# Small first loads and a four-part output store in a two-network block on one core

## The chip, the cores and the metric

The kernel runs on one core of one Trainium2 chip. The metric is the time of one execution in microseconds (us) on the device; the time of a version is the median of its runs. Names of engines in the profile: PE is TensorE's matmuls, PEld its weight loads, DVE is VectorE, ACT is ScalarE, POOL is GpSimd, SP is SyncE, which here issues all DMAs.

## The reference

The input x is 256 tokens by 1024 features, in float32. It goes through ten residual sublayers of one network and eight of a second one. Only the first and the last step matter for this change:

```python
for layer in range(2):
    x = x + 0.5 * swiglu(rmsnorm(x, ffn1_norm[layer]), ffn1_w_in[layer], ffn1_w_out[layer])
    ...                      # mixer (attention with a linear recurrence, then a delta rule),
                             # cross attention to a memory of 256 tokens, second swiglu
x = rmsnorm(x, final_norm)
for i in range(4):           # second network: retention, conformer convolution, GLA, retention
    ...
    h = h + rmsnorm_2(sq_relu_mlp(u, mlp_w_up[i], mlp_w_down[i]), norm_gains[i, 3])
```

swiglu is `(silu(gate) * up) @ w_out` with `gate, up = split(h @ w_in)`; rmsnorm divides by the root of the mean square over the features and multiplies by a gain. The first weight that is read is therefore `ffn1_w_in[0]`, the first gains are `ffn1_norm[0]`, and the last thing computed is x plus a normed MLP output.

## The kernel before, in words

**Layout.** Activations stand transposed: features on the 128 partitions, 8 chunks of 256 tokens side by side, so that x is one tile `X` of 128x2048 (chunk c is columns 256c to 256c+255). All weights are one list of 836 tiles of 128x1024, each made of four blocks of 128x256 in the order in which TensorE wants them. Tile t is loaded by SP into `SL[t % 3]`.

**Split precision.** Each product is made of three float32r products. ScalarE copies a tile to its rounded high part `WH[t % 4]` (`hi(t)`, L1981 to L1986), VectorE subtracts that from the original and gets the low part `WL[t % 4]` (`lo(t)`, L946 to L950). Activations are split likewise: `high` on ScalarE (L2053) and `low` on VectorE (L1012). TensorE takes block by block: high x high, high x low, low x high, each for two halves of 128 columns, six matmuls a block and 24 a tile (`multiply`, L293).

**Waits.** `tile` (L287) lets TensorE wait for `s_lo`, once every four blocks. `hi(t)` waits for the tile's DMA and, from the fifth tile on, for TensorE to be through with tile t-4. SP may load tile t when `lo(t-3)` is done. So the first three tiles have free buffers, and tile 3 is issued after `lo(0)`.

**Order of the start.** The first stage, `f1.0.in`, has 22 output groups of 8 blocks. Its first three groups are interleaved: for each chunk k of the input, blocks of groups 0, 1 and 2 (24 blocks, six tiles); from group 3 on the groups follow one another. ScalarE and VectorE run `walk_new` with n = 0 (L1999, L963): for each chunk c the split of the input chunk, and ahead of each even c one weight tile (tiles 0 to 3). Then the squares of the input for the norm (`square`, `add_squares`), and then `walk`, which handles tile b/4+3 at every fourth block b, so tile 4 comes right after the squares. Ahead of block (3, 0) TensorE sums the squares over the partitions (`total`), then ScalarE takes the root as exp(-0.5 ln) (`root`, L2041), for which `logs()` (L2021) loads an activation table. From there VectorE and ScalarE evaluate the swiglu groups as they are finished. Ahead of block (6, 0) TensorE transposes the memory (`mem_transposes`, L395) into three small banks in four lots; ScalarE empties these in `mem_copies` (L2157) when its own list has come there.

**Queues.** There is no planner: every engine has a list written out by hand. SP issues, in this order, the table of gains, biases and constants `PK` (128x1189, 594.5 KB), columns 0 to 1023 of x, weight tile 0, columns 1024 to 2047 of x, tiles 1 and 2, the memory (1 MB), then tiles 3 and 4, the positions, the constants `CP`, and the rest of the tiles (L2764 to L2783). TensorE, VectorE and ScalarE each wait for all of `PK` ahead of their first work (L914, L1962, L2718). At the end VectorE adds the last normed output to x chunk by chunk (`post_norm`, L1053), and SP waits for chunk 7, stores all of `X` with one DMA of 1 MB and waits for it (L2784 to L2786).

Of the kernel before, what the change touches and what calls it, by code (L numbers as in the profile page):

```python
# [109 lines left out]
def build_program(nc, w, pk, cp, xT_in, mem_in, pos_in, out):  # L110
    F32 = mybir.dt.float32
    I32 = mybir.dt.int32
    F32R = mybir.dt.float32r
    ALU = mybir.AluOpType
# [9 lines left out]
    with ctx:  # L124
# [47 lines left out]

        s_w = [sem(f"s_w{i}") for i in range(NRAW)]
        s_pk, s_mem, s_pos, s_cp, s_o = (sem(n) for n in ("s_pk", "s_mem", "s_pos", "s_cp", "s_o"))
        s_x = [sem(f"s_x{i}") for i in range(2)]
        s_hi, s_lo = sem("s_hi"), sem("s_lo")
        s_block, s_small = sem("s_block"), sem("s_small")
        s_bank = [sem(f"s_bank{i}") for i in range(8)]
# [81 lines left out]
        def tensor_program(p):  # L260
# [25 lines left out]

            def tile(st, j, k):  # L287
                b = st.at(j, k)
                if b % 4 == 0:
                    p.wait_ge(s_lo, b // 4 + 1)  # L290
                return WH[b // 4 % 4], WL[b // 4 % 4], b % 4 * 256

# [100 lines left out]
                to_x(f + ".out", 8 if n == 7 else None, RB, R03, hid_lo, f)  # L393

            def mem_transposes():  # L395
                p.wait_ge(s_mem, 16)
                for tb in range(2):
                    for q in range(2):
                        bk = small(("mem", tb, q))
                        for c in range(4):  # L400
                            at = tb * 1024 + (4 * q + c) * 128
                            t = p.transpose(bk[:, c * 128:(c + 1) * 128], PG[4][:, at:at + 128], IDN)
                        t.then_inc(s_small, 1)
# [507 lines left out]
                to_x("g.o", 18, R45, R45, o_lo, "g", 0, 2048)  # L911
                total(18)

            p.wait_ge(s_pk, 16)  # L914
            p.wait_ge(ones.sem, ones["ones"])
            for layer in range(2):
                n = 4 * layer
# [27 lines left out]
        def vector_program(v):  # L945
            def lo(t):  # L946
                if t < NTILES:
                    v.wait_ge(s_hi, t + 1)
                    v.tensor_tensor(WL[t % NSPL][:, :], SL[t % NRAW][:, :], WH[t % NSPL][:, :].bitcast(F32),  # L949
                                    ALU.subtract).then_inc(s_lo, 1)  # L950

            def walk(name, n=None, skip=0):

                st = ST[name]
                for x, (j, k) in enumerate(st.order):
                    b = st.block + x * st.width
                    if b and b % 4 == 0 and x >= skip:
                        lo(b // 4 + 3)
                    yield j, k
                    if n is not None and not st.outer and (j, k) == (0, 3):  # L960
                        add_squares(n, 3)

            def walk_new(name, n, chunk):  # L963

                t = ST[name].block // 4 + 3
                if n == 0:
                    for c in range(8):
                        if c % 2 == 0:
                            lo(c // 2)
                        chunk(c)  # L970
                else:
                    for c in range(8):
                        chunk(c, t + c // 2 - 2 if c in (4, 6) else None)
                    lo(t + 2)
                add_squares(n, 1)
                add_squares(n, 2)
                if n:
                    lo(t + 3)
                add_squares(n, 3)
                for j, k in walk(name, None, 16 if n else 0):  # L980
                    yield j, k
# [105 lines left out]
            def swiglu(f, n, gain, chunk=None):  # L1087
                name = f + ".in"
                for j, k in (walk(name, n) if n else walk_new(name, n, chunk)):
                    if n == 0 and (j, k) == (9, 3):  # L1090
                        mem_scaled()
                    for x in due(name, j, k, n > 0):
                        if x == 0:
                            v.wait_ge(s_rst, n + 1)
                        u = x // 2
                        s = Y8[:, u % 2 * 512:u % 2 * 512 + 512]
                        d = PG[10][:, u % 4 * 512:u % 4 * 512 + 512]
                        bk, free = done(name, x)
                        if x % 2 == 0:
                            v.tensor_tensor(r3(s), r3(bk[:, :]), RB2, ALU.mult).then_inc(free, 1)  # L1100
                            if u:
                                hid_low(f, u - 1)
                            continue
                        v.tensor_tensor(r3(d), r3(bk[:, :]), RB2, ALU.mult).then_inc(free, 1)
                        evacuated(name, x)
                        v.wait_ge(silu.sem, silu[f, u])
                        v.tensor_tensor(d, d, s, ALU.mult).then_inc(hid.sem, hid.give((f, u)))  # L1107
                hid_low(f, 10)
                if n == 7:
                    for j, k in walk(f + ".out"):  # L1110
                        rotary(0, j, k)
                        out_group(f + ".out", j, k, 8, 0.5, None)
                    return
                add_to_x(f + ".out", n + 1, 0.5, gain)
# [844 lines left out]
                return post_norm(18, 2, 1, gain)  # L1959

            v.memset(ONES[:, :], 1.0).then_inc(ones.sem, ones.give("ones"))
            v.wait_ge(s_pk, 16)  # L1962
            for layer in range(2):
                n = 4 * layer
                swiglu(f"f1.{layer}", n, gains("mix", 8 * layer), lambda c: low(0, c, gains("ffn1")))
# [14 lines left out]
        def scalar_program(a):  # L1980
            def hi(t):  # L1981
                if t < NTILES:
# [2 lines left out]
                        a.wait_ge(s_block, 4 * (t - NSPL + 1))  # L1985
                    a.activation(WH[t % NSPL][:, :], SL[t % NRAW][:, :], ACT.Copy).then_inc(s_hi, 1)  # L1986

            def walk(name, n=None, skip=0):

                st = ST[name]  # L1990
                for x, (j, k) in enumerate(st.order):
                    b = st.block + x * st.width
                    if b and b % 4 == 0 and x >= skip:
                        hi(b // 4 + 3)
                    yield j, k
                    if n is not None and (j, k) == ((3, 0) if st.outer else (0, 7)):
                        root(n)

            def walk_new(name, n, chunk):  # L1999

                t = ST[name].block // 4 + 3
                for c in range(8):
                    if n == 0 and c % 2 == 0:
                        hi(c // 2)
                    if n and c in (4, 6):
                        hi(t + c // 2 - 2)
                    chunk(c)
                square(n, 0, X[:, hc(0)])
                square(n, 1, X[:, hc(1)])
                if n:  # L2010
                    hi(t + 2)
                square(n, 2, X[:, hc(2)])
                square(n, 3, X[:, hc(3)])
                if n:
                    hi(t + 3)
                for x, (j, k) in enumerate(walk(name, n, 16 if n else 0)):
                    if n == 17 and x in (16, 20):
                        whole(n, range(x - 16, x - 12), gains("ng", 64))
                    yield j, k
# [20 lines left out]

            def root(n):  # L2041
                to = 258 if n in TOK else 256
                if n < 8:
                    logs()
                a.wait_ge(s_sums, n + 1)
                a.activation(RST[:, 0:to], BK[7][:, 0:to], ACT.Ln, bias=pc("eps"), scale=1.0 / 1024).then_inc(s_bank[7], 1)  # L2046
                a.wait_ge(s_bank[7], n + 1)
                a.activation(RST[:, 0:to], RST[:, 0:to], ACT.Exp, scale=-0.5).then_inc(s_rst, 1)
# [80 lines left out]

            def first_norm():  # L2130
                def chunk(c):
                    if c in (0, 4):
                        a.wait_ge(s_x[c // 4], 16)
                    high(0, c, gains("ffn1"))
                return chunk

# [578 lines left out]
                    pass  # L2715
                return post_norm(18, gain)

            a.wait_ge(s_pk, 16)  # L2718
            chunk = first_norm()
            for layer in range(2):  # L2720
                n = 4 * layer
# [5 lines left out]
            for i in range(4):  # L2727
                gain = gains("ng", (4 * i + 2) * 8)
                if i % 3 == 0:
                    chunk = retention(i, gain, chunk)  # L2730
                else:
                    chunk = (conformer, gla)[i - 1](gain, chunk)
                chunk = mlp(i, gains("ng", (4 * i + 4) * 8) if i < 3 else None, chunk)

        def sync_program(s):
            T0 = ST["dn.k"].block // 4
# [24 lines left out]
                    for b in range(8):  # L2761
                        s.dma_start(diagonal((PG[5], PG[4])[x], b), apart(DY, b, 256 * x)).then_inc(s_dn_y[x], 16)

            s.dma_start(PK[:, :], pk).then_inc(s_pk, 16)  # L2764
            s.dma_start(X[:, 0:1024], xT_in[:, 0:1024]).then_inc(s_x[0], 16)
            again = {ST["f2.0.in"].block // 4 + 8: (1, "xo0"), ST["f2.1.in"].block // 4 + 8: (2, "xo1"),
                     ST["m1.up"].block // 4 + 8: (3, "r0.o"), ST["m2.up"].block // 4 + 8: (2, "g.o")}
            for t in range(NTILES):
# [4 lines left out]
                blocks_of_16(t)  # L2773
                if t >= NRAW:
                    s.wait_ge(s_lo, t - NRAW + 1)
                s.dma_start(SL[t % NRAW][:, :], w[t]).then_inc(s_w[t % NRAW], 16)
                if t == 0:
                    s.dma_start(X[:, 1024:2048], xT_in[:, 1024:2048]).then_inc(s_x[1], 16)
                if t == 2:
                    s.dma_start(PG[4][:, :], mem_in[0]).then_inc(s_mem, 16)  # L2780
                if t == 4:
                    s.dma_start(POS[:, :], pos_in).then_inc(s_pos, 16)
                    s.dma_start(CP[:, :], cp[0]).then_inc(s_cp, 16)  # L2783
            s.wait_ge(xn.sem, xn[NN - 1, 7])  # L2784
            s.dma_start(out, X[:, :]).then_inc(s_o, 16)
            s.wait_ge(s_o, 16)  # L2786

        block_ = ctx.enter_context(nc.Block())

# [169 lines left out]
```

## Time and profile before

| | us |
|---|---|
| median of three runs | 2836.77 |
| the three runs | 2827.97, 2836.77, 2836.91 |
| span of the profiled execution, first to last instruction | 2834.6 |
| PE busy / DVE busy / ACT busy in that span | 2717.1 / 1812.7 / 1411.2 |

The profiled execution's own time is known only as its span; the median of the runs lies 2.2 us above it. TensorE is busy in 96% of the span, so time is made or lost in the few places where it stands idle, and at both ends. "Busy" of PE does not say at which clock it runs; the granted clock, 1.00 for full, is a separate column. In the profile a row's "idle before" names how long the engine stood idle and whose work ended that.

### The profile page before, as it was taken

How to read it: one execution, taken by the hardware profiler on the slowest of the kernel's cores; microseconds unless marked ns; L12 is line 12 of the kernel's file. 1: busy time of each engine (PE TensorE's matmuls, PEld its weight loads, DVE VectorE, ACT ScalarE, POOL GpSimd, SP SyncE). 2: the span in 40 equal slices, each digit the busy share in tenths (PEclk: the TensorE clock that was granted, in tenths of full speed). 3: DMA queues.
4: the chain of work that ended last, by engine and by line, in shares of the span. 5: the costliest groups of instructions: out<-in, count | busy, mean ns of one | idle time of the engine just before them, and what ended most of it. 6: DMA issues, size and time to landing. Idle time of an engine off the chain costs nothing. (4 is left out here: it accounts for less than half of the span.)

```text
span 2834.6 us, 49287 instructions
## 1 busy us (share of the span) xinstructions
PE 2717.1 (96%) x21142; PEld 2620.1 (92%) x21142; DVE 1812.7 (64%) x2351; ACT 1411.2 (50%) x1928; POOL 0.2 (0%) x4
## 2 busy tenths in 40 slices
PE   7999999999998899999999999989999999999998
PEld 7999899999987889999999999979988899989998
DVE  5658656656657746666746855967554685755764
ACT  5445545454456354545446565354454544446443
POOL 0000000000000000000000000000000000000000
PEclk9999999999999999999999999999999999999999
DMA  6554535555543133555544454135542455444463
GB/s 215 178 186 142 176 123 190 191 182 188 182 147 120 68 121 135 180 189 169 179 149 149 166 193 170 68 96 184 193 149 97 149 197 188 155 163 148 151 200 127
DMA packets 129002, 450.13 MB, mean 159 GB/s; under 512 B 20112, under 2 KB 20368, under 8 KB 128528
## 3 DMA queue, kind: packets, MB, share of 16 engines
q1 hardware_dynamic: 128784, 446.96, 47.0%
q8 instruction: 168, 2.75, 0.4%
q14 instruction: 50, 0.41, 0.0%
HBM read 445.47 MB, written 1.44 MB: 158 GB/s over the span
## 5 line engine op out<-in xcount | busy, mean ns | idle before, releaser
L262 PE MATMUL B<-R,WH 128*128 128x256 f32 x10432 | 2089.1, 283 | 45.5 <-DVE WL L949 28.4
L262 PEld LDWEIGHTS B<-R,WH 128*128 128x128 f32 x10432 | 1674.9, 189 | 63.6 <-issue 25.4
L949 DVE TENSOR_TENSOR WL<-SL,WH 128x1024 fp32r<-128x1024 f32 x836 | 1011.0, 1223 | 769.3 <-ACT WH L1986 768.1
L262 PE MATMUL B<-R,WL 128*128 128x256 f32 x4480 | 1255.1, 280 | 0.0
L1986 ACT ACTIVATE WH<-SL 128x1024 fp32r<-128x1024 f32 x836 | 865.9, 1052 | 567.5 <-PE B L262 442.5
L262 PEld LDWEIGHTS B<-R,WL 128*128 128x128 f32 x4480 | 845.7, 189 | 0.0
L262 PE MATMUL B<-RB,WH 128*128 128x256 f32 x1984 | 555.0, 280 | 0.0
L262 PE MATMUL B<-RB,WL 128*128 128x256 f32 x1728 | 482.7, 279 | 0.0
L262 PEld LDWEIGHTS B<-RB,WH 128*128 128x128 f32 x1984 | 372.2, 188 | 0.4
L262 PEld LDWEIGHTS B<-RB,WL 128*128 128x128 f32 x1728 | 323.8, 187 | 0.0
L262 PE MATMUL B<-WH,R 128*128 128x512 f32 x480 | 160.3, 403 | 1.3 <-DVE WL L949 1.3
L262 PE MATMUL B<-PG 128*128 128x256 f32 (+6 forms) x672 | 129.6, 337 | 8.8 <-DVE PG L1437 3.8
L262 PEld LDWEIGHTS B<-PG 128*128 128x128 f32 (+2 forms) x672 | 105.9, 187 | 22.8 <-issue 4.8
L2495 ACT ACTIVATE RB<-PG 128x512 fp32r<-128x512 f32 x64 | 40.5, 633 | 159.7 <-DVE PG L1583 159.7
L2054 ACT ACTIVATE R<-X,PK 128x256 fp32r<-128x256 f32 x128 | 61.4, 505 | 116.0 <-DVE X L1023 63.4
L262 PEld LDWEIGHTS B<-WH,R 128*128 128x128 f32 x480 | 90.7, 189 | 27.4 <-issue 3.5
L262 PE MATMUL B<-PG,ONES 128*128 128x256 f32 (+1 forms) x242 | 72.5, 422 | 30.7 <-DVE PG L990 15.0
L262 PE MATMUL B<-WL,R 128*128 128x512 f32 x240 | 95.2, 397 | 0.0
L2150 ACT ACTIVATE RB<-PG 128x512 fp32r<-128x512 f32 x44 | 27.8, 632 | 129.2 <-DVE PG L1107 129.2
L262 PEld LDWEIGHTS B<-PG,ONES 128*128 128x128 f32 x242 | 42.6, 195 | 41.0 <-issue 24.3
L1015 DVE SCALAR_TENSOR_TENSOR R<-X,PK,R 128x256 fp32r<-128x256 f32 x128 | 59.0, 482 | 28.7 <-ACT R L2054 28.7
L1038 DVE TENSOR_TENSOR R<-PG,RB 128x512 fp32r<-128x512 f32 x108 | 73.9, 685 | 3.3 <-ACT RB L2150 2.8
(282 smaller groups left out, 1541.2 us busy)
## 6 DMA issues: line engine op xcount, KB each, us to landing
SL<-in_w SPq DMA_DIRECT2D x836, 512.0 KB, 3.5
CP<-in_cp SPq DMA_DIRECT2D x5, 768.0 KB, 5.7
X<-in_xT SPq DMA_DIRECT2D x2, 512.0 KB, 6.9
PG<-in_mem SPq DMA_DIRECT2D x1, 1024.0 KB, 11.2
out<-X SPq DMA_DIRECT2D x1, 1024.0 KB, 3.9
PK<-in_pk SPq DMA_DIRECT2D x1, 594.5 KB, 3.8
dn_y<-PG SPq DMA_DIRECT2D x1, 256.0 KB, 2.3
PG<-dn_y SPq DMA_DIRECT2D x16, 16.0 KB, 2.2
```

The source lines that it names most:

```text
L262: return p.matmul(o, left, right, start=first, stop=final, skip_group_check=True)
L949: v.tensor_tensor(WL[t % NSPL][:, :], SL[t % NRAW][:, :], WH[t % NSPL][:, :].bitcast(F32), ALU.subtract).then_inc(s_lo, 1)
L1015: v.scalar_tensor_tensor(R67[:, 2048 + c * 256:2304 + c * 256], X[:, cc(c)], gain(c), R67[:, cc(c)].bitcast(F32), ALU.mult, ALU.subtract). ...
L1038: v.tensor_tensor(R03[:, hc(u)], d, RB[:, hc(u)].bitcast(F32), ALU.subtract).then_inc(hid_lo.sem, hid_lo.give((f, u)))
L1986: a.activation(WH[t % NSPL][:, :], SL[t % NRAW][:, :], ACT.Copy).then_inc(s_hi, 1)
L2054: a.activation(R67[:, cc(c)], X[:, cc(c)], ACT.Copy, scale=gain(c)).then_inc(h_hi.sem, h_hi.give((n, c)))
L2150: a.activation(RB[:, hc(u)], PG[10][:, u % 4 * 512:u % 4 * 512 + 512], ACT.Copy).then_inc(hid_hi.sem, hid_hi.give((f, u)))
L2495: a.activation(RB[:, hc(x)], PG[10][:, x % 4 * 512:x % 4 * 512 + 512], ACT.Copy).then_inc(hid_hi.sem, hid_hi.give((f, x)))
```

## The change

The first loads are cut up and put in another order, the waits for them with them, and the output is stored in four parts.

- SP first loads block 0 of tile 0 (128x256, 128 KB), then the 16 columns of `PK` that hold the first norm's gains (8 KB), then the other three blocks of tile 0 (384 KB), tile 1, the second half of x, tile 2, the rest of `PK`, the memory.
- ScalarE issues three DMAs itself, for chunk 0, chunk 1 and chunks 2 and 3 of x, then loads the logarithm's activation table (`logs()`), then waits for the gains. `root(0)` no longer loads that table.
- Tile 0 is split in two parts, block 0 and blocks 1 to 3, each with its own high and low instruction; TensorE waits for `s_lo_first` ahead of block 0, and for `s_lo` ahead of block 1.
- The waits for all of `PK` move to where its other columns are read: `mem_transposes`, `root(0)`, and VectorE's first `swiglu` group.
- The output goes in four DMAs, chunks 0 to 3, 4 and 5, 6, and 7, each when its last chunk is added.

```diff
@@ tensor_program @@
-                if b % 4 == 0:
+                if b == 0:
+                    p.wait_ge(s_lo_first, 1)
+                elif b == 1 or b % 4 == 0:
                     p.wait_ge(s_lo, b // 4 + 1)
...
             def mem_transposes():
+                p.wait_ge(s_pk, 16)
                 p.wait_ge(s_mem, 16)
...
-            p.wait_ge(s_pk, 16)
             p.wait_ge(ones.sem, ones["ones"])
@@ vector_program @@
+            def lo_part(part, needs, gives):
+                v.wait_ge(needs, 1)
+                v.tensor_tensor(WL[0][:, part], SL[0][:, part], WH[0][:, part].bitcast(F32), ALU.subtract).then_inc(gives, 1)
...
                 if n == 0:
-                    for c in range(8):
+                    lo_part(slice(0, 256), s_hi_first, s_lo_first)
+                    chunk(0)
+                    lo_part(slice(256, 1024), s_hi, s_lo)
+                    chunk(1)
+                    for c in range(2, 8):
                         if c % 2 == 0:
                             lo(c // 2)
                         chunk(c)
...
                             v.wait_ge(s_rst, n + 1)
+                            if n == 0:
+                                v.wait_ge(s_pk, 16)
...
-            v.wait_ge(s_pk, 16)
+            v.wait_ge(s_gain, 16)
@@ scalar_program @@
+            def hi_part(part, needs, gives):
+                a.wait_ge(needs, 16)
+                a.activation(WH[0][:, part], SL[0][:, part], ACT.Copy).then_inc(gives, 1)
...
+                if n == 0:
+                    hi_part(slice(0, 256), s_w_first, s_hi_first)
                 for c in range(8):
-                    if n == 0 and c % 2 == 0:
+                    if n == 0 and c == 1:
+                        hi_part(slice(256, 1024), s_w[0], s_hi)
+                    if n == 0 and c and c % 2 == 0:
                         hi(c // 2)
...
-                if n < 8:
+                if 0 < n < 8:
                     logs()
+                if n == 0:
+                    a.wait_ge(s_pk, 16)
...
-                    if c in (0, 4):
-                        a.wait_ge(s_x[c // 4], 16)
+                    if c in (0, 1, 2, 4):
+                        a.wait_ge(s_x[(0, 1, 2, 4).index(c)], 16)
...
-            a.wait_ge(s_pk, 16)
+            for x in range(3):
+                at = slice(XCUT[x], XCUT[x + 1])          # XCUT = (0, 256, 512, 1024, 2048)
+                a.dma_start(X[:, at], xT_in[:, at]).then_inc(s_x[x], 16)
+            logs()
+            a.wait_ge(s_gain, 16)
@@ sync_program @@
-            s.dma_start(PK[:, :], pk).then_inc(s_pk, 16)
-            s.dma_start(X[:, 0:1024], xT_in[:, 0:1024]).then_inc(s_x[0], 16)
+            s.dma_start(SL[0][:, 0:256], w[0][:, 0:256]).then_inc(s_w_first, 16)
+            s.dma_start(PK[:, 0:16], pk[:, 0:16]).then_inc(s_gain, 16)
+            s.dma_start(SL[0][:, 256:1024], w[0][:, 256:1024]).then_inc(s_w[0], 16)
...
-                s.dma_start(SL[t % NRAW][:, :], w[t]).then_inc(s_w[t % NRAW], 16)
-                if t == 0:
-                    s.dma_start(X[:, 1024:2048], xT_in[:, 1024:2048]).then_inc(s_x[1], 16)
+                if t:
+                    s.dma_start(SL[t % NRAW][:, :], w[t]).then_inc(s_w[t % NRAW], 16)
+                if t == 1:
+                    s.dma_start(X[:, 1024:2048], xT_in[:, 1024:2048]).then_inc(s_x[3], 16)
                 if t == 2:
+                    s.dma_start(PK[:, 16:NPK], pk[:, 16:NPK]).then_inc(s_pk, 16)
                     s.dma_start(PG[4][:, :], mem_in[0]).then_inc(s_mem, 16)
...
-            s.wait_ge(xn.sem, xn[NN - 1, 7])
-            s.dma_start(out, X[:, :]).then_inc(s_o, 16)
-            s.wait_ge(s_o, 16)
+            for c0, c1 in OUT:                            # OUT = ((0, 4), (4, 6), (6, 7), (7, 8))
+                s.wait_ge(xn.sem, xn[NN - 1, c1 - 1])
+                s.dma_start(out[:, c0 * 256:c1 * 256], X[:, c0 * 256:c1 * 256]).then_inc(s_o, 16)
+            s.wait_ge(s_o, 16 * len(OUT))
```

## Rows read from the trace of the kernel before

**Rows 1.** The page, part 1: busy us, share of the span, instructions.

```profile
PE 2717.1 (96%) x21142; PEld 2620.1 (92%) x21142; DVE 1812.7 (64%) x2351; ACT 1411.2 (50%) x1928; POOL 0.2 (0%) x4
```

**Rows 2.** Waits, whole span: waiter, releaser, us in total, times, longest.

```profile
PE B L262 <- DVE WL L949: 29.6, 27, 12.7
...
PE B L402 <- ACT PG L2161: 4.3, 1, 4.3
```

**Rows 3.** Timeline of SP's start: start us, us, what, [idle before <-releaser].

```profile
0.73 0.38 SPq L2764 DMA_DIRECT2D PK<-in_pk  x1
...
3.93 0.50 SPq L2780 DMA_DIRECT2D PG<-in_mem  x1
12.56 2.26 SPq L2776 DMA_DIRECT2D SL<-in_w  x2
```

**Rows 4.** Timeline of ACT, 0 to 54 us.

```profile
8.85 1.28 ACT L1986 ACT_TABLE_LOAD   x1 [8.85 <-DMA SL<-in_w]
...
17.05 1.06 ACT L1986 ACTIVATE WH<-SL 128x1024 fp32r<-128x1024 f32 x1 [1.56 <-DMA SL<-in_w]
...
20.90 1.05 ACT L1986 ACTIVATE WH<-SL 128x1024 fp32r<-128x1024 f32 x1
...
32.75 1.28 ACT L2022 ACT_TABLE_LOAD   x1
34.05 0.47 ACT L2046 ACTIVATE RST<-B,PK 128x256 f32<-128x256 f32 x1
...
53.97 1.55 ACT L2161 ACTIVATE PG<-B 128x512 f32<-128x512 f32 x3
```

**Rows 5.** Timeline of DVE, 22 to 52 us.

```profile
22.73 1.22 DVE L949 TENSOR_TENSOR WL<-SL,WH 128x1024 fp32r<-128x1024 f32 x1
...
51.05 0.68 DVE L1104 TENSOR_TENSOR PG<-B,RST 128x512 f32<-128x512 f32 x1
```

**Rows 6.** Timeline of PE, 22 to 55 us.

```profile
22.94 0.40 PE L262 MATMUL B<-R,WH 128*128 128x256 f32 x2
...
31.42 0.59 PE L262 MATMUL B<-PG,ONES 128*128 128x256 f32 x2
...
54.60 1.12 PE L402 MATMUL B<-PK,PG 128*128 128x128 f32 x4 [4.32 <-ACT PG L2161]
```

**Rows 7.** Stretches: length, busy (instructions) by engine, granted PE clock, DMA share, GB/s.

```profile
12.00:16.45 4.45, 3.77 (x18) 3.80 (x19) 4.45 (x8) 3.49 (x7) 0.00 (x0) 1.00 0.89 338
22.00:50.00 28.00, 28.00 (x239) 27.95 (x238) 18.62 (x22) 16.75 (x19) 0.00 (x0) 1.00 0.56 186
...
1043.00:1047.00 4.00, 4.00 (x24) 4.00 (x23) 1.97 (x5) 1.93 (x3) 0.00 (x0) 0.61 0.37 131
```

**Rows 8.** Stretches of one us, same columns.

```profile
13.00:14.00 1.00, 1.00 (x6) 1.00 (x6) 1.00 (x2) 1.00 (x3) 0.00 (x0) 1.00 0.70 279
```

**Rows 9.** The page, part 6: KB of one DMA, median us from issue to landing.

```profile
PG<-in_mem SPq DMA_DIRECT2D x1, 1024.0 KB, 11.2
out<-X SPq DMA_DIRECT2D x1, 1024.0 KB, 3.9
...
dn_y<-PG SPq DMA_DIRECT2D x1, 256.0 KB, 2.3
PG<-dn_y SPq DMA_DIRECT2D x16, 16.0 KB, 2.2
```

**Rows 10.** Weight tiles' DMAs in the first 40 us.

```profile
DMA to landing us min/median/max: 3.4/4.3/9.3
```

**Rows 11.** Timeline of DVE and SP at the end.

```profile
2829.89 0.42 DVE L1063 TENSOR_TENSOR X<-X,PG 128x256 f32<-128x256 f32 x1
2830.35 0.34 SPq L2785 DMA_DIRECT2D out<-X  x1
```

**Rows 12.** Timeline of PE, two later idle times.

```profile
1042.75 0.50 PE L262 MATMUL B<-R,WH 128*128 128x256 f32 x2 [2.18 <-DVE WL L949]
...
2222.99 0.46 PE L262 MATMUL B<-PG,ONES 128*128 128x256 f32 x1 [3.00 <-DVE PG L990]
```

More of the change, by code:

```diff
@@ L174, in build_program @@
         s_pk, s_mem, s_pos, s_cp, s_o = (sem(n) for n in ("s_pk", "s_mem", "s_pos", "s_cp", "s_o"))
-        s_x = [sem(f"s_x{i}") for i in range(2)]
+        s_x = [sem(f"s_x{i}") for i in range(4)]
+        XCUT = (0, 256, 512, 1024, 2048)
+        s_gain, s_w_first, s_hi_first, s_lo_first = (sem(n) for n in ("s_gain", "s_w_first", "s_hi_first", "s_lo_first"))
         s_hi, s_lo = sem("s_hi"), sem("s_lo")
@@ L2733, in scalar_program @@
                 chunk = mlp(i, gains("ng", (4 * i + 4) * 8) if i < 3 else None, chunk)
+        OUT = ((0, 4), (4, 6), (6, 7), (7, 8))
         def sync_program(s):
```

## The prediction

> **What bounds the kernel now.** I read the busy shares first [rows 1]: TensorE is busy for 2717.1 of 2834.6 us, so at most 117 us are to be had from its idle time, and both ends of the kernel are part of that. The waits come next [rows 2]: 29.6 us are spent waiting for VectorE's low parts of weights, and the longest of those waits, 12.7 us, is the start; the other 26 share 17 us and the change does not touch them. The one wait for ScalarE's copies of the transposed memory (L402) costs 4.3 us and matters below. Then the timelines of each engine at both ends.
>
> At the start the reader should see two things. TensorE begins at 12.7, because ScalarE waits until 8.85 for tile 0, behind the 594.5 KB of PK and half of x, and then loads a table for 1.28 us that nobody needs to wait for [rows 3, 4]. And once it has begun, it is never short of weights until 50 us (28.00 us busy in 28.00) [rows 7]. So the question is how soon TensorE would run short if it began sooner.
>
> **The start: how much of the earlier begin is kept.** When does it begin? The smallest loads of the trace land 2.2 to 2.3 us after issue [rows 9]. SP's first issue stands at 0.73 [rows 3]; block 0, the gains and chunk 0 should be there near 3.5. ScalarE's three issues (0.4 us each, as SP's) and the table load end near 3.3, so the load is hidden. High part, low part and the input's split of 128x256 are about 0.5 us each: first matmul near 5, one block, then a pause for blocks 1 to 3. These wait for 384 KB behind the small pieces, near 6.5, and for about 0.8 us of high and 0.9 us of low part (three quarters of 1.06 and 1.22): near 8.5. So TensorE begins 4 us earlier for good, by its own inputs.
>
> When does it run short? Weight tile 3 can't come much sooner. It stands behind the same 4.3 MB as before (PK, x, tiles 0 to 2, memory): the memory landed at 3.93 + 11.2 = 15.1 [rows 3, 9], and tile 3, issued at 12.56 after lo(0), was taken up by ScalarE at 17.05, on arrival [rows 3, 4]. What changes is that lo(0) is done about 4 us earlier, so tile 3 is queued right behind the memory; in the microsecond after 13 the DMAs showed a dip to 0.70 of their share [rows 8], which that closes. I take 0.5 us for it; the bounds are -1 (small rows and a second queue cost more than the dip) and +1.1 (12.56 + 3.4 = 15.96, the fastest landing of a tile in this stretch [rows 10]).
>
> Behind tile 3 there is a fixed list. ScalarE does hi(3), two input chunks, four squares, hi(4); VectorE does lo(3), two chunks, the sums of squares, lo(4), which ends at 22.73 + 1.22 = 23.95, that is 6.9 us after hi(3) started [rows 4, 5]. VectorE was without a pause in it. So lo(4) ends at 23.95 - 0.5 = 23.45 in the new kernel whatever TensorE does. TensorE began tile 3 at 22.94 and the sums at 31.42, three tiles later [rows 6]: 2.83 us each, and tile 4 at 25.77. In the new kernel, from block 1 at 8.5: about 3.8 us at half rate, as now (18 matmuls in 3.77 us, against 239 in 28.00 [rows 7]; the granted clock reads 1.00 in that first stretch, but 0.21 us a matmul against 0.117 is the engine's lower level, 1.2 of 2.4 GHz), then full rate, tile 3 would be wanted at 18.2; lo(3), 2.3 us behind its hi, is there near 18.9. Tile 4 would be wanted at 21.7 and is there at 23.45. From there tiles 5 and up were ready 2.7 us and more ahead of their use, so TensorE isn't held again. Gain at the start: 25.77 - 23.45 = **2.3 us**, not the 4 to 8 of the earlier begin. It doesn't depend on the exact begin: blocks 1 to 3 could start at 10 and tile 4 would still be waited for. Bounds 0.8 and 2.9 from those of tile 3. Cutting tile 0's high and low parts in two adds a fixed cost of some 0.3 us to each engine before 9, hidden in the wait for tile 3.
>
> **The table load.** root(0) loses the load at 32.75: the logarithm ran at 34.05 [rows 4], so it can start 1.30 us sooner, measured from TensorE's sums. From there ScalarE and VectorE work one behind the other and behind TensorE until 54 us: group 5 is scaled by VectorE at 51.05 [rows 5], while TensorE had finished it (it is the last before the transposes) near 49. The copies start at 53.97 [rows 4] and free the bank that TensorE has waited for for 4.32 us [rows 6]. No step of that chain waits for TensorE or a load by less than 1.3 us, as far as I follow it, so the whole **1.3 us** comes off this wait. Bounds 0 (one such wait found) and 1.3. After 54.6 everything follows TensorE again. No new load replaces it, since copies and squares need none of their own: at the end squares and the logarithm run with one table.
>
> On its price the Trainium skill differs (ScalarE: Activation LUTs, "What ACT_TABLE_LOAD costs"): it gives 1.28 us for the load and 1.38 for a drain, 2.66 in all. The trace shows the load and no drain: 32.75 to 34.05. By the page the term would be 2.7, by the trace 1.3.
>
> **Waits for PK** move behind 586 KB loaded before the memory, thus there before 15; their users come at 32 (root), 33 (first group) and 49. Cost nothing; if PK came after the memory instead, still nothing. Behind the moved wait on ScalarE stand root and all copies of weights, so only a landing past 32 would cost.
>
> **The end.** VectorE adds chunk 7 at 2829.89; the store is issued at 2830.35 and lands 3.9 us later [rows 9, 11], near the end of the span. Each chunk takes VectorE 0.86 us, so parts 1 to 3 are issued 3.4, 1.7 and 0.86 us before the last; an issue costs 0.34, so SP is free for each. The last part is 128 KB. 256 KB landed in 2.3 us, 16 KB in 2.2 [rows 9]: I take 2.3, so **1.6 us** less. Bounds: 0.5 (3.4, the fastest half megabyte [rows 10]) and 1.7.
>
> Of that the Trainium skill says (DMA: Bandwidth & Descriptors, "Anatomy of one DMA"), for another issuing path, that a DMA takes 2.0 us plus its bytes at 436 GB/s: 4.4 us for 1 MB, 2.3 for 128 KB, which would be a term of 2.1; the trace's 3.9 is below that. Its advice to batch DMAs speaks against small pieces; this is weighed in the bound of -1 above.
>
> **Sum.** 2.3 + 1.3 + 1.6 = 5.2 us: span 2834.6 - 5.2 = 2829.4, and with the 2.2 us between span and median 2836.77 - 5.2 = **2831.6**. About 0.3%, 8.5 us, is what a measurement of this kernel can tell from no change: its own three runs spread over 8.9 us. So the forecast is a gain inside that bound.
>
> **Rivals.**
> (a) Supply sooner: the DMAs moved 279 GB/s in the dip and 338 around it [rows 7, 8], and could run faster in the new order, so that tile 3 lands before 15 and TensorE sets its own pace: tile 4 at 21.7, start gain 4.1, in all 7.0: 2829.8. Against: the same bytes stand ahead. Chance 0.12.
> (b) The clock falls in the new pauses. TensorE now pauses near 18.5 and, for 1.7 us, before 23.45. After an idle time of 2.18 us at 1042.75 the granted clock read 0.61 in the next 4 us, with 24 matmuls where 34 fit [rows 7, 12]: 1.2 us lost there, 1.6 with its edges. This would leave 0.7 of the start's 2.3: 2833.2. For: the pauses are of that length; against: 3.00 us of idle at 2222.99 were followed by full pace (matmuls 0.117 apart), so idle time alone doesn't decide. Chance 0.2. The Trainium skill (TensorE: Matmul & The Clock Gate, Part 1) has the same two levels and says that the point at which the clock changes varies from run to run, which no single trace can show.
> (c) The pieces land no sooner than before, or the load stays: only the end's 1.6 and part of the rest, 2834. Chance 0.1.
> (d) Slower: the same gate further on. Everything after 55 us comes 3.6 us earlier, and in this execution about six idle times of 1.8 us or more went without a fall (2222.99 is one) while six others brought one. Each that changes sides costs 1.6, as above, to 2.8, the longest of the trace. From four more on (6.4 to 11) the gain is used up: 2838 to 2843. It must be a majority in one direction, and just as likely the other way. Chance 0.08.
> The forecast itself keeps 0.5.
>
> **Numbers.** One run of three lay 8.9 us below the others, which (d)'s mechanism would explain (five falls fewer), and it may strike the new kernel too. A median of three lands in the low state with 3 x (1/3)^2 x (2/3) + (1/3)^3 = 0.26, giving 2823. So faster by over 0.3%: 0.25 (this, and a little of (a)); slower by over 0.3%: 0.04 from (d); within: 0.71. Range 2822 to 2838: the low state below, (c) and the light end of (d) above; the forecast's own range, from the bounds of the three terms (1.3 to 5.9), is 2830.9 to 2835.5.
>
> **What would show it.** First matmul near 5, dense from 8 to 9. ScalarE takes tile 3 at 16 to 17, waiting for its DMA. A TensorE wait of 1 to 2 us for lo(4) near 22 to 23.5, none before the transposes. The logarithm right behind hi(9), and the wait at L402 down from 4.3 to 3.0. Last store landing 2.2 to 2.4 after issue. Wrong if tile 4 isn't waited for (then (a)), if matmuls near 20 to 28 stand 0.21 apart (b), or if L402's wait stays at 4.3.

## The result and the profile after

Over 20 runs of each, the changed kernel took 2832.53 us in the median (2816.96 to 2839.08) and the kernel before 2838.94 (2827.97 to 2848.4). The ratio is 0.9977, with a 95% interval of 0.9966 to 0.9988: 6.5 us less, between 3.4 and 9.7. The forecast was 5.2 us less. Both the sign and the size came out, but one of the three terms, the start, did not, as this section and the experiments show.

The timeline of ScalarE in the changed kernel's first 55 us (start, duration, engine, line, operation, idle time before it and what ended that) shows the start:

```profile
2.12 1.28 ACT L2044 ACT_TABLE_LOAD   x1 [2.12 <-issue]
...
8.65 0.84 ACT L2004 ACTIVATE WH<-SL 128x768 fp32r<-128x768 f32 x1 [3.60 <-DMA SL<-in_w]
...
17.74 1.06 ACT L2000 ACTIVATE WH<-SL 128x1024 fp32r<-128x1024 f32 x1 [3.42 <-DMA SL<-in_w]
...
31.32 1.06 ACT L2000 ACTIVATE WH<-SL 128x1024 fp32r<-128x1024 f32 x1 [0.32 <-DMA SL<-in_w]
32.29 0.45 ACT L2070 ACTIVATE RST<-B,PK 128x256 f32<-128x256 f32 x1
```

The table load is out of the way at 3.4 and no second one precedes the logarithm, which starts right behind the high part of tile 9: both as forecast. But the rest of tile 0 was taken up at 8.65 (forecast 6.5), and tile 3 at 17.74, later than the 17.05 of before [rows 4] and not sooner. The last tile ahead of the root, tile 9, was waited for as well, at 31.32. Tile 3 was late, and the first loads had run slower than in the kernel before. The first seven microseconds, before and then changed (length, busy time and instructions of PE, PEld, DVE, ACT and POOL, granted clock, DMA share, GB/s):

```profile
0.00:7.00 7.00, 0.00 (x0) 0.00 (x0) 0.17 (x1) 0.00 (x0) 0.20 (x4) 1.00 0.67 208
```

```profile
0.00:7.00 7.00, 1.62 (x6) 1.36 (x6) 0.98 (x3) 2.10 (x3) 0.20 (x4) 1.00 0.54 155
```

53 GB/s less over 7 us are 0.37 MB; at the 407 to 413 GB/s that the DMAs moved between 13 and 19 us these cost 0.9 us. Tile 3 was late by 0.7 us, which is of that size. TensorE's timeline has the same points from its side:

```profile
5.34 0.55 PE L264 MATMUL B<-R,WH 128*128 128x256 f32 x1 [5.34 <-DVE WL L958]
10.54 0.79 PE L264 MATMUL B<-R,WH 128*128 128x256 f32 x2 [3.58 <-DVE WL L958]
...
24.69 0.50 PE L264 MATMUL B<-R,WH 128*128 128x256 f32 x2 [1.20 <-DVE WL L953]
52.83 1.12 PE L407 MATMUL B<-PK,PG 128*128 128x128 f32 x4 [3.52 <-ACT PG L2185]
```

It starts at 5.3 instead of 12.7, works densely from 10.5, pauses for tile 4 until 24.69 (forecast 23.45; it began that tile at 25.77 before), and goes on after the transposes at 52.83, against 54.60 [rows 6]: 1.8 us sooner, where 3.6 were forecast.

Why tile 9 was late although TensorE came sooner, SP's list shows. SP may load tile 9 when `lo(6)` is done, and `lo(6)` follows hi(6), for which TensorE need only be through with tile 2. So in this stretch the issue doesn't wait for TensorE. Its issue in the kernel before, and in the changed one:

```profile
27.18 0.33 SPq L2776 DMA_DIRECT2D SL<-in_w  x1
```

```profile
26.93 0.33 SPq L2808 DMA_DIRECT2D SL<-in_w  x1
```

It landed 4.3 us later before, at 31.5, just ahead of TensorE's release of hi(9) at 31.68, and 4.4 us later in the changed kernel, at 31.3. TensorE reached the sums 1.0 us sooner (30.45, against 31.42 [rows 6]), but tile 9 was issued only 0.25 us sooner.

At the end, VectorE's last sum, and what each size of store took to land (page, part 6, for that stretch):

```profile
2822.19 0.42 DVE L1075 TENSOR_TENSOR X<-X,PG 128x256 f32<-128x256 f32 x1
```

```profile
out<-X SPq DMA_DIRECT2D x1, 512.0 KB, 2.6
out<-X SPq DMA_DIRECT2D x1, 256.0 KB, 2.5
out<-X SPq DMA_DIRECT2D x2, 128.0 KB, 1.9
```

The span ends at 2824.9, 2.3 us after that sum; before it was 2834.6 - 2830.3 = 4.3 [rows 11]. So the store gave 2.0 (forecast 1.6): 128 KB land in 1.9 us, less than the 2.3 that I took from 256 KB.

1.8 and 2.0 make 3.8. The two profiled executions differ by 9.7. The other 5.9 lie between 54.6 and the last sum, where no instruction was changed. Most of it lies in places like this one, as stretches in the same columns, of the changed kernel and then of the kernel before:

```profile
1160.00:1280.00 120.00, 120.00 (x1062) 120.00 (x1061) 83.66 (x94) 58.33 (x67) 0.00 (x0) 1.00 0.60 197
```

```profile
1160.00:1280.00 120.00, 120.00 (x1021) 120.00 (x1021) 80.83 (x90) 55.74 (x66) 0.00 (x0) 1.00 0.55 182
```

TensorE is busy throughout in both, at a granted clock of 1.00, and yet does 4% more matmuls in one: 0.113 us apart instead of 0.1175. The changed kernel's profile holds 30 stretches of 10 us with 90 or 91 matmuls, the other none. That is chance or the change's doing; the experiments had to tell.

### The profile page after: what moved, and what is told of

It is laid out like the page before. It is cut to its first block and busy times, and to the rows that moved or that the text cites. A ratio compares the mean times of both kernels' runs of the same rounds, so it can differ in the third digit from the quotient of the medians.

```text
span 2824.9 us, 49296 instructions
## 1 busy us (share of the span) xinstructions
PE 2712.5 (96%) x21142; PEld 2614.1 (93%) x21142; DVE 1811.8 (64%) x2352; ACT 1409.3 (50%) x1928; POOL 0.2 (0%) x4
## 5 line engine op out<-in xcount | busy, mean ns | idle before, releaser
L264 PE MATMUL B<-PG,ONES 128*128 128x256 f32 (+1 forms) x242 | 73.4, 426 | 29.5 <-DVE PG L1002 13.7
L2174 ACT ACTIVATE RB<-PG 128x512 fp32r<-128x512 f32 x44 | 27.8, 632 | 128.8 <-DVE PG L1121 128.8
```

The costliest lines, as they stand in the source:

```text
L264: return p.matmul(o, left, right, start=first, stop=final, skip_group_check=True)
L2174: a.activation(RB[:, hc(u)], PG[10][:, u % 4 * 512:u % 4 * 512 + 512], ACT.Copy).then_inc(hid_hi.sem, hid_hi.give((f, u)))
```

## The experiments

Eleven experiments were run; three of them are repeats, two of the changed kernel and one of the cut loads alone. The first four shared one chip and one set of runs of the kernel before. The next four ran on another chip with a second set, and the last three on that chip with a third. Where two versions are compared by their mean times, the number after +- is one standard error.

**The four-part store alone**, on the kernel before:

```diff
-            s.wait_ge(xn.sem, xn[NN - 1, 7])
-            s.dma_start(out, X[:, :]).then_inc(s_o, 16)
+            for c0, c1 in OUT:
+                s.wait_ge(xn.sem, xn[NN - 1, c1 - 1])
+                s.dma_start(out[:, c0 * 256:c1 * 256], X[:, c0 * 256:c1 * 256]).then_inc(s_o, 16)
```

> The kernel before with only the four-part store. Theory (the three terms add up, each in its own place): from the end of VectorE's last sum to the end of the span 2.3 us instead of 4.3, so 2.0 less; nothing else moves: TensorE goes on after the transposes at 54.6, as before. Rival (small stores wait for one another, and the gain of the changed kernel's end came from elsewhere): 3 us or more from the last sum to the end. Whole kernel by the theory -2.0 us, far inside the spread of runs, which I expect to come from the middle of the kernel: two profiled executions differ there by up to 5 us in single stretches at full granted clock.

Measured: last sum ends at 2837.45, span 2839.8, so 2.35 us; restart after the transposes at 54.27. Ratio 0.9993 (0.9978 to 1.0008). The term is 2.0 us and stands by itself; the rival is out.

**The table load alone**, on the kernel before:

```diff
-                if n < 8:
+                if 0 < n < 8:
                     logs()
...
+            logs()
             a.wait_ge(s_pk, 16)
             chunk = first_norm()
```

> The kernel before, with the logarithm's table loaded at ScalarE's start and not again ahead of the first root. Theory A (the load's price is 1.3 us wherever no load of weights holds ScalarE there): TensorE's restart after the transposes at 54.60 - 1.3 = 53.3, its wait 3.0 instead of 4.3. In the changed kernel it was 0.7, because ScalarE waited 0.3 us for tile 9's DMA just ahead. And the table load at the start goes out of the way of tile 0's high part too: ScalarE's first high part at 8.9 instead of 10.15, TensorE's start 1.3 earlier at 11.4; by theory B (tile 4 is not waited for in the kernel before, 1.8 us of slack) that start is kept whole as well: restart at 52.0. If tile 3 and its list bind, restart stays near 52.0 to 53.3. Rival C (the load at the root was hidden): restart at 54.6 less only the start's shift. Whole kernel -1.3 to -2.6 us.

Measured: start at 11.03, and TensorE's restart in the row below at 52.59, between the 53.3 of theory A and the 52.0 of theory B, its wait 2.89; the logarithm at 32.06. Ratio 0.9987 (0.9976 to 0.9999).

```profile
52.59 0.66 PE L402 MATMUL B<-PK,PG 128*128 128x128 f32 x4 [2.89 <-ACT PG L2161]
```

One line moved gives 2.0 us at the restart. From the start of hi(9) to the logarithm it is 0.97 us (31.09 to 32.06) instead of 2.37 (31.68 to 34.05): 1.4 for the load. The other 0.6 is hi(9) itself, 31.09 instead of 31.68, released by TensorE in both. TensorE had begun 1.65 us sooner, but its matmuls stood 0.21 us apart until 17.1 instead of 16.45, so a part of that was lost. The 2.0 us are more than all that the changed kernel gained at the restart (1.8, and 1.1 to 1.4 in its two repeats): on top of the moved table load, the cut loads made the restart 0.2 to 1.0 us later, not sooner.

**The cut loads alone**: the changed kernel with the single store and with the load ahead of the first root.

```diff
-                if 0 < n < 8:
+                if n < 8:
                     logs()
...
-            for c0, c1 in OUT:
...
+            s.wait_ge(xn.sem, xn[NN - 1, 7])
+            s.dma_start(out, X[:, :]).then_inc(s_o, 16)
```

> The changed kernel with the single store of 1 MB and with the table loaded again ahead of the first root: the cut loads alone. Theory A (start's gain 1.1 us, set by tile 3's landing at 17.7 and the fixed list behind it): TensorE waits for tile 4 until 24.7; restart after the transposes at 54.60 - 1.1 = 53.5. Rival (the load at the root is hidden by the wait for tile 9, so it costs nothing): restart at 52.8, as in the changed kernel. End: 4.3 us from the last sum, as before. Whole kernel by A -1.1 us.

Measured: TensorE waits for tile 4 until 24.40, near A's 24.7, and the end takes 4.3 us as before. But the restart is at 54.48, neither 53.5 nor 52.8: the cut loads alone gain nothing there. ScalarE's timeline says why:

```profile
31.55 1.06 ACT L2000 ACTIVATE WH<-SL 128x1024 fp32r<-128x1024 f32 x1 [0.31 <-DMA SL<-in_w]
32.63 1.28 ACT L2044 ACT_TABLE_LOAD   x1
33.92 0.47 ACT L2070 ACTIVATE RST<-B,PK 128x256 f32<-128x256 f32 x1
```

The reader should see that the root stands behind tile 9's DMA, at the time at which it stood before behind TensorE (31.68). As long as tile 9 is issued at 27.1, an earlier TensorE gains nothing. The first timing gave 0.9985 (0.9970 to 1.0000); that is taken up below.

**Fewer bytes ahead of the tiles.** The changed kernel with the rest of PK after tile 4 and the memory after tile 6:

```diff
-                if t == 2:
+                if t == 4:
                     s.dma_start(PK[:, 16:NPK], pk[:, 16:NPK]).then_inc(s_pk, 16)
+                if t == 6:
                     s.dma_start(PG[4][:, :], mem_in[0]).then_inc(s_mem, 16)
-                if t == 4:
+                if t == 16:
                     s.dma_start(POS[:, :], pos_in).then_inc(s_pos, 16)
```

> The changed kernel with the rest of PK issued after tile 4, the memory after tile 6, and positions and CP after tile 16. Theory A (the bytes ahead of tile 3 set the start's gain): 1.6 MB less stand ahead of tile 3, some 4 us at 400 GB/s, so ScalarE takes it near 14, lo(4) ends near 21, TensorE isn't held at tile 4 and reaches it at its own pace, 16 blocks from 10.5 with 3.8 us at half rate: near 23.6; restart after the transposes near 51.5 to 52.0, 1 us sooner than the changed kernel's 52.83. Rival B (the list of ScalarE and VectorE binds, not the landing): lo(4) at 24.6 as now, restart at 52.8. Rival C (the later loads collide with tiles 5 to 9): waits of TensorE for low parts after tile 4, restart later than 52.8. Whole kernel by A -7.5 us against before.

Measured: tile 3 taken up at 13.84 without a wait, no pause at tile 4, restart at 51.55. Theory A for tile 3. But the logarithm only moved to 31.01, since the memory's 1 MB now lay ahead of tile 7:

```profile
27.55 1.06 ACT L2000 ACTIVATE WH<-SL 128x1024 fp32r<-128x1024 f32 x1 [4.04 <-DMA SL<-in_w]
```

Ratio 0.9969 (0.9957 to 0.9980). So the collision had moved, not gone, and the next kernel moved the memory past tile 9.

**The memory after tile 12**, positions and CP after tile 20 (the same edit with `t == 12` and `t == 20`):

> The changed kernel with the rest of PK issued after tile 4, the memory after tile 12, positions and CP after tile 20. Theory A (TensorE's restart after the transposes stands 20.55 us behind the first root's logarithm in every trace so far, and the logarithm stands right behind the high part of tile 9, which waits for that tile's DMA): without the memory's 1 MB among tiles 7 to 9, hi(9) is released by TensorE at about 27, the logarithm starts near 28, restart near 48.5 to 49.5, which is 3 to 4 us sooner than the changed kernel's 52.83; whole kernel 7 to 9 us below before. Rival B (the start's pace is TensorE's or VectorE's, not the loads'): restart at 51.5, as with the memory after tile 6. Rival C (the memory lands too late for the transposes): a TensorE wait ahead of the transposes.

Measured: in ScalarE's timeline, tile 9 now waits for TensorE, and the logarithm stands at 29.94:

```profile
28.98 1.06 ACT L2000 ACTIVATE WH<-SL 128x1024 fp32r<-128x1024 f32 x1 [1.40 <-PE B L264]
```

SP issues tile 9 3.9 us sooner than in the changed kernel, and it lands 4.7 us later, at 27.8, 1.2 us before TensorE is through:

```profile
23.07 0.33 SPq L2808 DMA_DIRECT2D SL<-in_w  x1
```

Restart at 50.48, 2.4 us sooner than in the changed kernel; I had said 3 to 4, since I had TensorE 2 us too early at that tile. Median 2830.87, ratio **0.9959** (0.9944 to 0.9974). By the means it is 12.4 us below before, +- 1.9. This is the lowest ratio of all, but its interval overlaps those of the memory after tile 6 and of both edits together. The edit moves three loads at once, the rest of PK, the memory, and the positions with CP; which of them counts was not separated.

**The gains as 128 columns** (512 bytes a partition instead of 64), profiled once:

```diff
-            s.dma_start(PK[:, 0:16], pk[:, 0:16]).then_inc(s_gain, 16)
+            s.dma_start(PK[:, 0:128], pk[:, 0:128]).then_inc(s_gain, 16)
```

> The changed kernel with the first gains loaded as 128 columns of PK (512 bytes a partition, 64 KB) instead of 16 (64 bytes, 8 KB). Theory A (the short rows hold up the queue: in the changed kernel the DMAs moved 93 and 162 GB/s between 3 and 5 us, against 337 and 225 before): the rest of tile 0 lands 1 us or more sooner than 8.65, first matmul near 4.5, dense from near 9.5. Rival B (another reason for the slow microseconds, the second queue or the first accesses): first high part near 4.3 to 5, dense from 10.2 to 10.5 as now. By both the restart stays near 52.8, as tile 9's DMA sets it.

Measured: the rest of tile 0 at 7.67 (8.65 in the changed kernel), dense work from 9.55, restart at 52.30. The DMAs moved 189 GB/s in the first 7 us instead of 155, and tile 3 was taken up at 16.61, so tile 4 began at 23.57 and the sums at 29.12, 2.3 us sooner than before: here the start's gain on TensorE is what was forecast. Yet hi(9) waited for tile 9's DMA until 30.75, only 0.9 us sooner than before, so that the restart had 0.9 us of these 2.3, and 1.4 from the table load. The stretches of the fifth microsecond, first of this kernel, then of the changed one:

```profile
4.00:5.00 1.00, 0.00 (x0) 0.00 (x0) 0.00 (x0) 0.52 (x2) 0.00 (x0) 1.00 0.92 310
```

```profile
4.00:5.00 1.00, 0.00 (x0) 0.00 (x0) 0.23 (x1) 0.76 (x2) 0.00 (x0) 1.00 0.53 162
```

That fits theory A, but the profiles with the narrow gains took up the rest of tile 0 anywhere from 8.13 to 8.65, and the combined kernel below, with the wide gains too, only at 8.46. One profile doesn't settle a difference of that size.

**The memory after tile 12 in the kernel before**, profiled once, with the whole PK and x as before:

> The kernel before with the memory issued after tile 12, positions and CP after tile 20. Theory A (in the kernel before hi(9) waits for TensorE, not for a load): restart after the transposes unchanged at 54.3 to 54.6, logarithm at 33.7 to 34.05. Rival B (fewer bytes help whatever the start): restart 2 to 4 us sooner.

Measured: restart 54.75, logarithm 34.20, tile 9 released by TensorE. Theory A: late memory is worth nothing without the early start. The early start (the cut loads) is worth nothing without the late memory. Together they brought the restart 2.4 us ahead of the changed kernel's and 2.1 ahead of that with the table load alone. The late memory with the old start and the moved table load was not run.

**The changed kernel again**, profiled once:

> The changed kernel once more, for the spread. Theory A (the middle's 5.9 us between the two profiled executions was chance: 30 stretches of 10 us with 90 or 91 matmuls where all other traces have 87 or 88): restart near 52.8, end 2.3 us behind the last sum, but a middle of 2780 to 2784 us with few such stretches, as in the four experiments so far. Rival B (the change itself makes them): again near 30 of them, starting after 1159 and 1928, and a middle near 2770.

Measured: restart 53.18, 2.3 us at the end, and between them 2778.8 us with one fast stretch instead of 2769.8 with 30. Theory A, a little under its 2780.

**Both helpful edits together**, timed, and with it the changed kernel and the cut loads alone once more, to see whether the 3 us by which timed runs had gone beyond their terms were real:

> The changed kernel with both edits that helped: gains as 128 columns, the rest of PK after tile 4, the memory after tile 12, positions and CP after tile 20. Theory A (the logarithm is set by hi(9), which TensorE releases there, and TensorE's dense work starts with the landing of the rest of tile 0): dense start near 9.5 instead of 10.0, logarithm near 29.5 instead of 29.94, restart near 50.0. Rival (a load holds hi(9) again): restart 50.5 or later. Whole kernel by the profile's terms 4.6 + 2.0 = 6.6 us below before; if the unexplained 3 to 5 us that timed runs of kernels with the early start showed beyond their terms are real, 10 to 12.

> The changed kernel timed beside the others on one chip. Theory A (its terms add to 3.8 us: restart 1.4 to 1.8 sooner, end 2.0 shorter, and the rest is spread): difference of the means 3.8 +- 1.6, ratio 0.9987. Rival B (something in the middle gains as well, since 20 runs showed 6.0 +- 1.7 and a part of the experiments 3 us beyond their terms): 6 us or more again, ratio 0.9978 or less.

> The cut loads alone (single store, table loaded again ahead of the first root), timed once more. Theory A: its terms add to 0.1 us, so 0 +- 1.6 us, ratio 1.000. Rival B (the early start itself makes the middle shorter): 3 us or more, as the first time (3.2 +- 1.6 by the means), ratio 0.9989 or less.

Measured: both together 2831.54, ratio 0.9967 (0.9952 to 0.9982), restart 50.59, dense from 10.35, so the wide gains added nothing here. The restart is the rival's number but not its cause: TensorE, and no load, released hi(9) at 29.09, later than theory A had it. By the means this kernel is 8.4 us below before, +- 1.8. The changed kernel 0.9990 (0.9976 to 1.0003), by the means 3.0 us less, +- 1.5. The cut loads alone 1.0008 (0.9996 to 1.0021), by the means 1.1 more, +- 1.5. Theory A in both: for these two kernels the excess of the first timing did not come back. It is not gone from the whole table, though. "Terms" is the mean restart against the 54.5 of the kernels with the old start, plus 2.0 for the four-part store where it is in:

| kernel | terms, us | less than before, by the means |
|---|---|---|
| store alone | 2.0 | 2.5 +- 1.7 |
| table alone | 2.0 | 3.5 +- 1.4 |
| cut loads alone, first and second time | -0.2 | 3.2 +- 1.6, -1.1 +- 1.5 |
| changed, first and second time | 3.3 | 6.0 +- 1.7, 3.0 +- 1.5 |
| memory after tile 6 | 5.0 | 8.7 +- 1.3 |
| memory after tile 12 | 6.1 | 12.4 +- 1.9 |
| both | 6.0 | 8.4 +- 1.8 |

The two with late memory and narrow gains lie 3.7 and 6.3 us beyond their terms, about three standard errors each. One thing that the terms leave out is the clock behind the restart, told in the last section. In their profiles it is worth some 2.5 us to the table alone, the memory after tile 12 and both. The rest stays open.

All profiled executions side by side. "Rest" is the time from the restart to the end of the last sum; "fast" counts stretches of 10 us with 90 matmuls or more; the last column is the sum of (1 - granted clock) x length over the stretches up to 2800 us, so that the time behind the last matmul doesn't count:

| kernel | logarithm | restart | rest | fast | clock lost, us |
|---|---|---|---|---|---|
| before | 34.05 | 54.60 | 2775.7 | 0 | 18.9 |
| store alone | 33.71 | 54.27 | 2783.2 | 3 | 27.3 |
| table alone | 32.06 | 52.59 | 2780.2 | 3 | 23.8 |
| before, memory later | 34.20 | 54.75 | 2783.9 | 2 | 27.2 |
| cut loads alone | 33.92 | 54.48 | 2779.8 | 3 | 28.9 |
| cut loads alone, again | 34.43 | 54.99 | 2787.0 | 0 | 35.9 |
| changed | 32.29 | 52.83 | 2769.8 | 30 | 23.8 |
| changed, again | 32.62 | 53.18 | 2778.8 | 1 | 23.8 |
| changed, third | 33.01 | 53.55 | 2779.8 | 13 | 29.0 |
| memory after tile 6 | 31.01 | 51.55 | 2783.3 | 1 | 30.6 |
| memory after tile 12 | 29.94 | 50.48 | 2772.1 | 16 | 20.5 |
| wide gains | 31.71 | 52.30 | 2784.8 | 3 | 32.3 |
| both | 30.05 | 50.59 | 2780.9 | 1 | 27.2 |

From the logarithm to the restart it is 20.53 to 20.59 us in all thirteen. "Rest" varies over 17 us, follows no edit, and grows with the clock lost and falls with the fast stretches. Less the clock lost, and with 0.4 us added for each fast stretch (10 us with 4% more matmuls), it varies over 7 us. The three profiles with 13 or more fast stretches are all of kernels with the cut loads, three of nine against none of four; chance alone would give that about three times in ten, so a link is not shown.

## Why the prediction was right, and where it was not

- **The store: right, a little small.** 2.0 instead of 1.6, alone as in the whole. The size was off because 128 KB land in 1.9 us; the bound of 1.7 was passed.
- **The table load: right.** The logarithm follows hi(9) directly. From the start of hi(9) to it there are 1.4 us less than before (2.37 and 0.97). Comparing the cut loads alone with the changed kernel, the mean restart moves by 1.5 (54.48 and 54.99, against 52.83, 53.18 and 53.55). So the trace's price held, within 0.1 us. The Trainium skill's page ScalarE: Activation LUTs ("What ACT_TABLE_LOAD costs") gives 2.66 us with its drain; these runs don't agree.
- **The start: the failing step.** It was put as "Gain at the start: 25.77 - 23.45 = 2.3 us" and "TensorE isn't held again"; the cut loads alone gave 0 (54.48 and 54.99, against 54.27 to 54.75 in the three kernels with the old start). Two things failed in it. Its own size: tile 3 landed 0.7 later instead of 0.5 sooner (inside the bound of -1), so tile 4 began at 24.7, 1.1 sooner and not 2.3. The list behind tile 3 took its 6.9 us as forecast.

  And its passage, which counts for more, since with the wide gains TensorE did come 2.3 sooner and only 0.9 of it reached the root: I followed TensorE's slack tile by tile up to tile 5, but what sets the restart is the root on ScalarE, and that stands behind hi(9). Before, TensorE released hi(9) at 31.7 with the load ready since 31.5, a slack of 0.2 us (in the run of the store alone, tile 9 was waited for already, 0.36 us, at 31.33). As TensorE came sooner, it was the DMA of tile 9 that ended the wait. That load is issued after lo(6), and tile 6 in turn after lo(3): in this stretch the loads make a chain of their own that starts with tile 3 and doesn't wait for TensorE.

  I had written "no step of that chain waits for TensorE or a load by less than 1.3 us, as far as I follow it", and had followed it only behind the logarithm, not ahead of it. The late loads show it as the cause: with them tile 3 was taken up at 13.7 and tile 9 issued at 23.1, the same cut loads let TensorE release hi(9), and the restart came 2.4 us sooner.
- **What covered the error.** The terms come to 3.8 in the profiled pair, and to some 3.3 with the mean restart of the three profiles (53.2, against 54.5). The first 20 runs of each differ by 6.0 +- 1.7 in the means, the second set by 3.0 +- 1.5. Each is within two standard errors of 3.3. That the first fell so near to the forecast is in part luck. The lower end of the range rested on a low group of runs, seen once in three; the twenty runs of the kernel before, from 2828 to 2848, show no such group apart from the rest.
- **Rivals.** (a), tile 3 before 15, didn't occur, but the late memory made it occur, and its 7.0 us compares with the 6.1 that the restart and the end of that kernel add up to (12.4 +- 1.9 in the timed runs). (b), half rate after the new pause at tile 4, didn't occur: after 1.20 us of idle at 24.69 the matmuls stand 0.118 apart. (c) is what became of the cut loads, by another way: they landed sooner and it did not matter. (d): falls of the clock do differ from one execution to the next (19 to 36 us of clock lost), but they were not what made the profiled pair differ; the changed kernel had lost more, 23.8 against 18.9, and was still shorter in the middle, through its fast stretches.

## What to carry to other kernels

A start that comes sooner is worth what the last of its followers lets through. Don't stop at the first engine that is not held again; go on to the next place where several engines meet (here the first root), and ask what ended the wait there and how far behind the second cause was. When two causes end within a few tenths of a microsecond, take both away or neither: cut loads gave 0, late memory gave 0, together they gave 2.1 on top of the table load. Where buffers are refilled as they come free, follow the loads as a chain of their own, here from tile 3 by tile 6 to tile 9. And try the smallest edit by itself: the one moved table load did as much for the restart as the whole new start. And a load that isn't needed for 40 us doesn't belong among the first ones, nor just behind them: here it held up whatever was waited for next.

## What the runs showed of the hardware

- **Two paces of TensorE at full granted clock.** The same instructions run 0.1175 or 0.113 us apart, the faster pace for up to 140 us at a time, 4% of difference; 120 us of the faster pace is worth 5 us. Of thirteen profiles, two have 16 and 30 such stretches of 10 us, one 13, the others none to three. In the changed kernel two of these phases begin at a rise of the clock (1158.5) and behind a pause of 1.10 us (1927.97); in other executions they begin elsewhere. What decides it was not tested and stays open. With the clock lost, it accounts for most of the spread of 17 us in the profiles: 7 us are left without the two.
- **Falls of the clock come in steps.** Each fall is to a granted clock of 0.50, half of the full one, and a single fall costs 1.7, 3.4 or 5.1 us, in all thirteen profiles.
- **The pause at the transposes brought a fall or none.** In the three profiles in which TensorE had waited there 2.9 us (table alone, memory after tile 12, both), the granted clock stayed at 1.00 behind it. In the ten with 3.5 to 4.9 us it fell to 0.50 and cost 1.7 us in five and 3.4 in the other five. The changed kernel with its 3.52 us, then the memory after tile 12 with 2.89:

```profile
50.00:60.00 10.00, 7.17 (x48) 7.17 (x49) 2.90 (x3) 6.60 (x8) 0.00 (x0) 0.83 0.41 138
```

```profile
50.00:60.00 10.00, 9.52 (x81) 9.53 (x82) 4.55 (x5) 6.73 (x9) 0.00 (x0) 1.00 0.35 127
```

  Elsewhere length alone doesn't decide: 2.18 us at 1042.75 brought a fall and 3.00 at 2222.99 none [rows 12]. So in these profiles the shorter pause went with a gain beyond its own length; whether its length is the cause was not tested.
- **Small stores land soon.** 1.9 us for 128 KB, 2.5 for 256 KB, 2.6 for 512 KB, against 3.9 for 1 MB.
